# A two-block model step on one core: input reads of ScalarE spread out, its table loaded earlier, TensorE's first unit begun one column tile sooner

## The reference, cut to what matters

```python
u = rms_norm(h, norm_mix[i])                 # h = x, 512 x 1024
mix = diff_attention(u, attn_w_qkv[j], ...)  # begins with u @ w_qkv, 1024 x 3072
h = h + mix
h = h + squared_relu_mlp(rms_norm(h, norm_ffn[i]), ffn_w_up[i], ffn_w_down[i])
# then an S5 layer and an MLP, then a second block with convolution, attention and a gated FFN
```

## Time and profile before

| | |
|---|---|
| median of 3 runs | 1870.55 us (1868.81 to 1870.89) |
| the profiled execution: device time | 1867.82 us |
| its span | 1866.0 us |
| TensorE busy | 1786.5 us (96%) |
| VectorE busy | 1300.6 us (70%) |
| ScalarE busy | 778.5 us (42%) |
| mean granted TensorE clock | 0.984 |

### The profile page before, as it was taken

The page is one execution under the profiler, slowest core; times in us unless marked ns, Lnnn a source line. Parts: engine busy times, 40 slices in busy tenths (PEclk is TensorE's granted clock), DMA queues, the critical chain, the costliest instruction groups (busy, mean ns, idle before and its releaser), DMA issues.

```text
span 1866.0 us, 25467 instructions
## 1 busy us (share of the span) xinstructions
PE 1786.5 (96%) x9314; PEld 1438.1 (77%) x9314; DVE 1300.6 (70%) x2397; ACT 778.5 (42%) x1271; POOL 47.9 (3%) x39
## 2 busy tenths in 40 slices
PE   7999999999999992999999999999999999999998
PEld 6886688888888862888888788779755788888886
DVE  5868967767886669536655686458899976776465
ACT  5237944422342372424321342244687343333211
POOL 0000000000000000000000000000043100000000
PEclk9999999999999995999999999999999999999999
DMA  7320022444555489434444676224101223223532
GB/s 213 104 89 23 1 71 98 145 149 149 172 156 154 141 255 139 147 102 136 147 147 146 202 231 228 80 68 125 36 33 46 68 83 106 94 90 101 180 102 68
DMA packets 99928, 224.98 MB, mean 121 GB/s; under 512 B 19297, under 2 KB 48609, under 8 KB 99825
## 3 DMA queue, kind: packets, MB, share of 16 engines
q1 hardware_dynamic: 53520, 166.81, 29.2%
q10 hardware_dynamic: 46304, 56.77, 9.8%
HBM read 202.68 MB, written 20.87 MB: 120 GB/s over the span
## 4 chain that ended last, share of the span: by engine, by line
PE 90%; DVE 4%; SPq 2%; DMA 1%; ACT 1%; issue 1%; ACTq 0%; DVEq 0%
PE PS L444 26%; PE PS L446 26%; PE PS L445 26%; PE PS L637 2%; SPq L408 2%; PE PS L1024 1%; PE PS L662 1%; PE PS L998 1%; DMA Tm<-k_scratch 1%; PE PS L650 1%; PE PS L1032 1%; PE PS L561 1%; PE PS L818 1%; PE PS L504 1%; PE PS L1025 1%
## 5 line engine op out<-in xcount | busy, mean ns | idle before, releaser
L1657 DVE TENSOR_TENSOR WL<-raw,WH 128x1024 fp32r<-128x1024 f32 x228 | 279.6, 1231 | 275.0 <-ACT WH L1120 265.7
L1120 ACT CAST WH<-raw 128x1024 fp32r<-128x1024 f32 x228 | 237.3, 1046 | 489.0 <-PE PS L446 409.9
L444 PE MATMUL PS<-XH,WH 128*128 128x512 f32 x928 | 366.3, 395 | 4.5 <-issue 4.3
L446 PE MATMUL PS<-XH,WL 128*128 128x512 f32 x928 | 362.8, 391 | 0.0
L445 PE MATMUL PS<-XL,WH 128*128 128x512 f32 x928 | 362.6, 391 | 0.0
L444 PE MATMUL PS<-WH,AH 128*128 128x512 f32 x688 | 269.6, 392 | 0.0
L446 PE MATMUL PS<-WH,AL 128*128 128x512 f32 x688 | 267.9, 389 | 0.0
L445 PE MATMUL PS<-WL,AH 128*128 128x512 f32 x688 | 267.7, 389 | 0.0
L444 PEld LDWEIGHTS PS<-XH,WH 128*128 128x128 f32 x928 | 175.0, 189 | 42.9 <-issue 7.2
L444 PE MATMUL PS<-WH,XH 128*128 128x512 f32 (+2 forms) x512 | 197.3, 385 | 11.1 <-DVE XL L1728 10.4
L446 PEld LDWEIGHTS PS<-XH,WL 128*128 128x128 f32 x928 | 175.1, 189 | 37.2
(11 more groups left out here) (368 smaller groups left out, 2462.2 us busy)
## 6 DMA issues: line engine op xcount, KB each, us to landing
raw<-units_dram SPq DMA_DIRECT2D x272, 512.0 KB, 3.3
ada_late<-ada_units_dram ACTq DMA_DIRECT2D x48, 512.0 KB, 3.8
wi_scratch<-WIe ACTq DMA_DIRECT2D x16, 512.0 KB, 2.9
ca_scratch<-CAr ACTq DMA_DIRECT2D x32, 256.0 KB, 3.5
WI<-wi_scratch SPq DMA_DIRECT2D x16, 512.0 KB, 8.3
CA<-ca_scratch SPq DMA_DIRECT2D x16, 512.0 KB, 7.3
Tm<-k_scratch SPq DMA_DIRECT2D x8, 512.0 KB, 20.3
bc<-bc_dram ACTq DMA_DIRECT2D x16, 160.0 KB, 2.2
```

Source lines behind the costliest of these rows:

```text
L444: pe.matmul(o, lh, rh, start=start, stop=False)
L446: return pe.matmul(o, ll, rh, start=False, stop=stop)
L1120: nc.scalar.copy(WH[:, (u + n) % SLOTS], raw[:, s]).then_inc(hi_done, 1)
L1657: v.tensor_tensor(WL[:, s], raw[:, (u + n) % 2], WH[:, s].bitcast(F32), ALU.subtract).then_inc(unit_ready, 1)
```

## The change

Three edits, all in the first microseconds.

1. ACT issues x tile 0, g_mix, and x tiles 1 and 2. Tiles 3 and 4 are issued behind XH 1, tile 5 behind XH 2, tiles 6 and 7 behind XH 3.
2. Behind its first four issues ACT waits for `eps_set` and runs a one-element-per-partition Identity into the scratch tile `ew`. The table load stands ahead of that instruction.
3. TensorE takes unit 0 by column tile: 12 matmuls on column tile 0 after a wait for XL 0, then 12 on column tile 1 after a wait for XL 1. Before, one wait for both stood ahead of all 24.

```diff
@@ TensorE, chunk loop
                     if c >= 2:
                         pe.wait_ge(qk_ev, NT * (c - 1))
-                    token_chunk(UNITS["qkv"] + 4 * c, 4 * (1 - c % 2), XH, XL, ts=t_mix0 if c == 0 else None)
+                    if c == 0:
+                        pe.wait_ge(unit_ready, 1)
+                        for k in range(2):
+                            pe.wait_ge(t_mix0.lo, t_mix0.base + k + 1)
+                            for t in range(NT):
+                                m = three(psum(4 + t), XH[:, k, t * P:(t + 1) * P], XL[:, k, t * P:(t + 1) * P],
+                                          WH[:, 0, k * 512:(k + 1) * 512], WL[:, 0, k * 512:(k + 1) * 512], k == 0, False)
+                        m.then_inc(unit_used, 1)
+                    token_chunk(UNITS["qkv"] + 4 * c, 4 * (1 - c % 2), XH, XL, ts=t_mix0 if c == 0 else None, first=0 if c else 2)
@@ ScalarE
-                for k in range(KD):
-                    a.dma_start(XT[:, k, :], io["x_t"][k]).then_inc(wi_in[k], 16)
-                    if k == 0:
-                        a.dma_start(g_mix[:, :, :], io["norm_mix_col"]).then_inc(wi_in[0], 16)
+                def x_load(first, last):
+
+                    for k in range(first, last):
+                        a.dma_start(XT[:, k, :], io["x_t"][k]).then_inc(wi_in[k], 16)
+
+                x_load(0, 1)
+                a.dma_start(g_mix[:, :, :], io["norm_mix_col"]).then_inc(wi_in[0], 16)
+                x_load(1, 3)
+                a.wait_ge(eps_set, 1)
+                nc.scalar.activation(ew[:, 0, :], eps_rms[:, :], ACT.Identity)
...
                     nc.scalar.activation(XH[:, k, :], XT[:, k, :], ACT.Identity, scale=g_mix[:, 0, k:k + 1]).then_inc(t_mix0.scaled, 1)
+                    if k in (1, 2, 3):
+                        x_load((3, 5, 6)[k - 1], (5, 6, KD)[k - 1])
```

## The result

The changed kernel is slower: median 1876.63 us of 8 runs (1873.46 to 1880.4) against 1870.72 us of 8 runs before (1866.68 to 1875.15). The ratio of the runs is 1.0031 with a 95% interval of 1.0019 to 1.0042, so +3.6 to +7.9 us.

A forecast was written before the change was run, and what follows sets the result against it. TensorE, busy 96% of the span, was taken to bound the kernel: starting 2.0 us earlier, then standing 3.9 us ahead of unit 2, net +1.9 on the 1870.55 median, gives 1872.4; range 1868.0 to 1877.0.

The forecast's parts named there:

- line of 3.7 us: Whole kernel: a difference under 0.2%, 3.7 us, counts as none; slower than that got 0.22, same 0.75, faster 0.03.
- The earlier start: TensorE's first matmul: at 8.4 us in place of 10.44, gain 2.0 us, bounds 1.5 and 2.9.
- The use of unit 2's cover: TensorE at unit 2: wanted at 21.4, ready at 21.5 with nothing else changed, so the 1.9 us cover is used up.
- Tile 3 and the issue of tile 7: ACT's later x reads: tile 3 lands at 11.1, bounds 9.9 and 11.5; tile 7 is issued at 11.7.
- Tile 7's landing: Last x read: 4.7 us from issue, landing at 16.4, bounds 14.5 and 17.7; constants and unit 2's rounding queue behind it.
- The constants: Eleven constant reads on ACT ahead of unit 2's rounding: 6.5 us, against 7.8 before and 5.2 at the fastest pace.
- my bound of 27.9: TensorE beginning unit 2: forecast at 25.3 against 23.36 before, with bounds of 22.1 to 27.9.
- The clock: Rival: TensorE's clock falls in the 3.9 us stall before unit 2, costing 1.9 us, total +3.8, 1874.3; chance 0.25.
- 2 us of idleness do no harm: TensorE's clock: granted clock stayed at 1.00 in the idle stretch 1214 to 1216 us, so some more idleness may be harmless.
- The price of 1.9 us: Clock rival's cost, from TensorE's start: 9 matmuls took 3.98 us where 9 take 2.06 at 2.4 GHz.
- The thinnest cover in the first 60 us: Unit 2: ready at 21.5, wanted by TensorE at 23.36, a cover of 1.9 us, called the thinnest in that span.

The follow-up runs named there:

- e3: The changed kernel with SyncE waiting for XH of all eight tiles before issuing the reads into h; ratio to the kernel before 1.0025.
- e4: The changed kernel with 34 added matmuls of 128x512 between TensorE's units 1 and 2, into an unread PSUM bank; ratio to the kernel before 1.0019.
- e8: The changed kernel with the h reads replaced by same-size weight-unit reads, 128 rows of 2 KB; one execution, tile 7 landed at 17.07, stall 3.3 us.
- e1: The changed kernel with the reads of x tiles 3 to 7 issued straight behind the early Identity, beside the table load; ratio to the kernel before 1.0004.
- e2: The changed kernel with units 2 and 3 rounded ahead of the eleven constant reads; ratio to the kernel before 1.0004.

## Why the prediction was right in its direction and range, and where its sum was off

The forecast was 1872.4 us, +1.9; the measured difference of the medians is +5.9 and the time, 1876.63, lies in the range near its upper end. That the range held is luck in part. Unit 2 came later than its bound, and the clock fell as well; the profile shows +8.0 at attention, above the +6.4 at which the range ends, and only the medians stay inside. By the prediction's own line of 3.7 us the kernel is slower, to which it gave 0.22. By its own steps:

- **The earlier start** was forecast at 8.4 and came at 8.10. The limit was g_mix, as worked out: it landed at 6.4 and not 6.8. Right.
- **The use of unit 2's cover** was right: TensorE would have wanted unit 2 at 21.3, and stood.
- **Tile 3 and the issue of tile 7** were forecast at 11.1 and 11.7 and came at 11.5 and about 11.9. Right.
- **Tile 7's landing is the step that failed in size**: 4.7 us forecast with a bound of 5.7, measured 10.4. The prediction took rope_sin's 4.1 us as a row "in just that company". It was not: rope_sin was issued at 11.79, just ahead of the first read into h, and tile 7 is issued behind it. The constants that were issued behind the first h read in the same trace took 5.1 us (gq, issued at 12.30), 7.3 (gk, at 12.78) and then 8.4 to 11.2, though they are small; these were the nearest rows. From the kernel before, the h reads and three of these constants (subln was issued at 15.09):

```profile
11.83 6.41 SPq L381 DMA_DIRECT2D h<-x_in_dram  x8
```
```profile
gq<-q_gain_dram ACTq DMA_DIRECT2D x1, 32.0 KB, 5.1
gk<-k_gain_dram ACTq DMA_DIRECT2D x1, 32.0 KB, 7.3
subln<-subln_col_dram ACTq DMA_DIRECT2D x1, 0.5 KB, 11.2
```

  Of the 5.7 us that were missing about 3 are the h reads in front (e3 without them 7.1 us, e4 ahead of them 6.8). The other 2.4 are there without any h read (e3), and their cause stays open. How much the low rate of the h reads adds is not shown, since in e8 tile 6 was issued ahead of them all.
- **The constants** were forecast at 6.5 us and took 5.2, my lower bound.
- Together: tile 7 landed 5.9 us late (22.3 against 16.4), the constants gave 1.3 back, so unit 2 came at 29.87 in place of 25.3, outside my bound of 27.9.
- **The clock** stood as a rival with 1.9 us and a chance of 0.25. With the longer stall it became the case: 1.5 to 2.6 us in the two profiles, 1.6 by e4. The Trainium skill (TensorE: Matmul & The Clock Gate, on the HAM clock gate) says that an idle TensorE falls to half rate; the trace agrees. The prediction's reading that 2 us of idleness do no harm does not hold. Its row of 1214 to 1216 us ends too soon: TensorE waited 2.3 us there, and the next row of the same view shows the clock at half:

```profile
1216.00:1218.00 2.00, 1.75 (x4) 1.49 (x5) 2.00 (x5) 0.43 (x1) 0.00 (x0) 0.52 0.00 0
```

  It also fell behind a stall of 2.1 us (e1) and one of 3.3 (e8, 0.50 from 27 us), and not with one of 2.7 (e2), so the length of the stall alone does not tell. The price of 1.9 us was read from the pace of the first matmuls (0.43 us each), where the granted clock reads 1.00; the pace behind the stalls at 0.50 is the same 0.43.
- **"The thinnest cover in the first 60 us"** was wrong. Chunk 2 at 56.0 had less: none. It did not matter for the changed kernel, as its loss came earlier and had nothing to fall back on, but it is why undoing the harm (e1) did not bring the 2 us, and I would have seen it had I set the eviction's end beside TensorE's arrival.

Still open: the profiles put the changed kernel 7.6 to 8.4 us behind at attention, the medians only 5.9 (interval 3.6 to 7.9). The stage that waits for Tm moves by some us in both kernels: its first matmul is at 735.1 and 737.0 before, 747.0 and 744.8 after. Whether it gives something back on the mean, these runs don't tell.

## What to carry to other kernels

A start-up gain is worth no more than the next cover behind it, and the one behind that: list for the first units when each is ready and when TensorE wants it, for evictions too, before pricing an earlier start. A read that is put behind a wait loses its place in the queue, and what it then costs depends on what has got in front (tile 7 took 6.8 us ahead of the h reads and 9.4 to 10.4 behind them); keep critical reads ahead of bulk reads, and issue them beside a table load rather than after it. Work that needs no late data (here the rounding of a weight unit) should not stand behind a wait for late data or behind a row of DMA issues.

## What the runs showed of the hardware

- ScalarE's DMA issues run beside its table load: in e1 the first three of the five reads were issued from 2.83 to 4.25, the load ran from 2.76 to 4.04.

```profile
2.76 1.28 ACT L1110 ACT_TABLE_LOAD   x1 [2.76 <-issue]
2.83 1.42 ACTq L1104 DMA_DIRECT2D XT<-x_t_dram  x3
```

- Full DMA engines are not full bandwidth: from 16 to 20 us, while reads of 64 rows of 4 KB at a 32 KB stride were the bulk, the changed kernel moved 214 to 236 GB/s where e8, with 128 rows of 2 KB, moved 400 GB/s, both at a DMA share of 1.05 to 1.08. e8 changes the number of rows, and with it the number of partitions written (64 to 128), their length, their stride and the tensor read together; which of them counts was not tried, and e8 is one execution.
- The eleven issues of small reads take 7.8 us beside SyncE's issues and 5.2 us alone, as 0.48 each.
